# Two output projections of a two-layer trunk as three fp32r products, with weights split by Pool and expert reads moved

## What is computed

```
def diff_attend(q, k, v, lam):
    s = jnp.einsum('cbhqd,cbhkd->cbhqk', q, k)
    p = jax.nn.softmax(s, axis=-1)
    a = p[0] - lam * p[1]
    return jnp.einsum('bhqk,bhkd->bhqd', a, v)

def finish(o):                          # layer 0
    o = rms_norm(o, subln_g) * (1.0 - lambda_init)
    return o.transpose(0, 2, 1, 3).reshape(b, n, D_MODEL) @ w_o

y_lat = o.transpose(1, 0, 3, 2, 4).reshape(b, n, D_MODEL) @ w_o    # layer 1

x = x + gate * y ; h = modulate(rms_norm(x)) ; x = x + gate2 * moe_ffn(h)
```

## Time and profile before

| | |
|---|---|
| median of 3 runs | 1168.38 us (1167.69 to 1175.12) |
| the profiled execution | 1169.04 us, span 1167.2 us |
| mean granted TensorE clock | 0.942 |
| PE busy | 979.8 us, 84% |
| DVE, ACT, POOL busy | 410.1, 365.0, 217.7 us |
| transferred | 321.68 MB, mean 276 GB/s |

### The profile page before, as it was taken

One profiled execution on the slowest core, in us unless ns is written; L12 is line 12 of the kernel. 1 busy time (PEld: TensorE's weight loads), 2 busy tenths in 40 slices (PEclk: granted clock), 3 DMA queues, 4 the chain that ended last, 5 costly groups with the idle time before them and its releaser, 6 DMA issues.

```text
span 1167.2 us, 24449 instructions
## 1 busy us (share of the span) xinstructions
PE 979.8 (84%) x9618; PEld 664.6 (57%) x9619; DVE 410.1 (35%) x840; ACT 365.0 (31%) x777; POOL 217.7 (19%) x329
## 2 busy tenths in 40 slices
PE   4899999988799979799899659999999677996651
PEld 1577777544455655467676447887555545773331
DVE  1533330357843532122222273312853621221113
ACT  3532222456831222122222354223851210220011
POOL 0000000000000034244344301910000132442221
PEclk9899999989999999899999969999999898998786
DMA  9866664998230658999999467223527789999982
GB/s 339 280 225 223 223 216 175 337 362 302 105 161 36 235 213 359 423 418 424 426 421 416 173 240 177 75 72 112 249 75 313 303 336 420 401 423 423 426 374 114
DMA packets 92962, 321.68 MB, mean 276 GB/s; under 512 B 21289, under 2 KB 33234, under 8 KB 80610
## 3 DMA queue, kind: packets, MB, share of 16 engines
q1 hardware_dynamic: 85026, 305.00, 67.7%
q0 software_dynamic: 7008, 12.62, 3.0%
q10 hardware_dynamic: 864, 3.15, 0.7%
HBM read 313.28 MB, written 13.99 MB: 280 GB/s over the span
## 4 chain that ended last, share of the span: by engine, by line
PE 67%; DMA 16%; DVE 6%; issue 5%; ACT 3%; SPq 1%; POOL 1%; POOLq 0%; DVEq 0%; ACTq 0%
PE ps L1947 22%; PE ps L1713 21%; DMA expert_sets<-in_moe_w_up_dram 12%; PE ps L1868 7%; PE ps L1610 5%; PE ps L1634 4%; PE ps L1768 2%; DMA ring<-in_ada_w_dram 2%; PE ps L1795 1%; PE ps L1824 1%; DMA expert_rows<-moe,scatter_idx 1%; DMA val<-expert_rows 1%; PE ps L1651 1%; PE ps L1746 1%; ACT hT L951 1%
## 5 line engine op out<-in xcount | busy, mean ns | idle before, releaser
L1947 PE MATMUL ps<-expert_sets,moe 128*32 128x256 f32 x6304 | 368.1, 393 | 82.8 <-DMA expert_sets<-in_moe_w_up_dram 42.0
L1947 PEld LDWEIGHTS ps<-expert_sets,moe 128*32 128x32 f32 x6304 | 248.2, 114 | 201.9 <-issue 102.0
L1537 DVE STREAM_TRANSPOSE moe<-moe 128x256 f32<-128x256 f32 x70 | 45.7, 654 | 301.3 <-PE ps L1947 283.8
L1713 PE MATMUL ps<-w_high,x_high 128*128 128x512 f32 x352 | 142.2, 404 | 6.8 <-DVE x_low L489 5.1
L1713 PE MATMUL ps<-w_high,x_low 128*128 128x512 f32 x352 | 139.1, 395 | 0.0
L1713 PE MATMUL ps<-w_low,x_high 128*128 128x512 f32 x352 | 139.0, 395 | 0.0
L1090 ACT ACTIVATE moe<-ps 128x128 f32<-128x128 f32 x68 | 18.9, 277 | 308.5 <-PE ps L1947 304.1
L476 DVE TENSOR_TENSOR w_low<-ring,w_high 128x2048 fp32r<-128x2048 f32 x24 | 57.0, 2383 | 133.1 <-ACT w_high L473 133.1
L759 POOL MEMSET moe<- 128x128 f32 x2 | 0.4, 204 | 541.7 <-PE ps L1894 541.7
L783 POOL DMA_INDIRECT expert_rows<-moe,scatter_idx x74 | 75.8, 1024 | 82.8 <-POOL scatter_idx L820 55.2
L1713 PEld LDWEIGHTS ps<-w_high,x_high 128*128 128x128 f32 x352 | 67.2, 191 | 30.7 <-issue 17.6
(11 more groups left out here) (241 smaller groups left out, 1115.8 us busy)
## 6 DMA issues: line engine op xcount, KB each, us to landing
expert_sets<-in_moe_w_down_dram SPq DMA_DIRECT2D x32, 2048.0 KB, 21.8
expert_sets<-in_moe_w_gate_dram SPq DMA_DIRECT2D x30, 2048.0 KB, 17.1
expert_sets<-in_moe_w_up_dram SPq DMA_DIRECT2D x30, 2048.0 KB, 22.8
ring<-in_ada_w_dram SPq DMA_DIRECT2D x16, 2048.0 KB, 8.1
ring<-in_diff_w_qkv_dram SPq DMA_DIRECT2D x6, 2048.0 KB, 8.7
ada_late<-in_ada_w_dram SPq DMA_DIRECT2D x6, 2048.0 KB, 12.1
ring<-in_na_w_qkv_dram SPq DMA_DIRECT2D x6, 2048.0 KB, 8.8
val<-expert_rows SPq DMA_DIRECT2D x12, 512.0 KB, 4.5
```

The costliest lines, as they stand in the source:

```text
L1537: dve.transpose(blk_inT, blk_in[b].rearrange("p (j k) -> p k j", k=KC)).then_inc(m_xt[l], 1)
L1713: mm = pe.matmul(ps[:, n % 2], x_part[:, k, tok], w_part, start=(k == 0 and i == 0), stop=(k == KC - 1 and i == 2))
L1947: mm = pe.matmul(ps[g * SLOTS:(g + 1) * SLOTS, bank, 0:n_out], lhs_T[:, k, :], weights(k, g), start=(k == 0), stop=(k == n_chunks - 1), sk ...
```

## The change

In both layers the product with w_o becomes three fp32r products for each chunk. POOL splits each strip of w_o in halves: a copy to wo_high (fp32r, over expert set 0) and a subtraction into w_low (in place, over the ring). In layer 0 it starts behind the last modulation products, in layer 1 behind the last QKV product. The heads are split too: in layer 0 ACT's copy writes heads_high, and DVE's new heads_low writes x_low from the same bank, one tile ahead; PE may turn the next tile only when heads_low is through. In layer 1 scale_out gets a rounding copy and a subtraction for each pair of heads. As wo_high and heads_high lie where expert 0's weights go, SP reads expert 0 behind the last products of the projection, in both layers, ahead of expert 2. The softmax of layer 0's first half isn't divided by its sum: the combine is e0 + (lam * s0 / s1) * e1, one wide DVE operation instead of two, and the factor 1 / s0 goes into the head's norm by four small operations on the statistics. No other stage is changed.

```
+        wo_high = over("wo_high", SET_KB[0], [P, 2, KC, STRIP], F32R)
+        heads_high = over("heads_high", SET_KB[0] + 32, [P, KC, TILES * P], F32R)
+        o_low = over("o_low", H_KB, [P, KC, SEQ], F32R)
+        first_sums = stat[:, 3]
@@ SP, load_experts
                     expert_weights(l, w, 1, 1)
+                for w, value in ((0, 2 * NT[l] - 1), (1, 2 * NT[l]), (2, 2 * NT[l])):
+                    sp.wait_ge(s_wm[l], value)
+                    expert_weights(l, w, 0, 0)
                 for w, used, value in ((0, s_wm, 2 * NT[l] - 1), (1, s_wm, 2 * NT[l])):
@@ SP, behind layer 0's QKV and behind layer 1's
-            for w, used, value in ((0, s_ada, 2 * ADA - 1), (1, s_ada, 2 * ADA), (2, s_adt, 2 * ADA)):
-                sp.wait_ge(used, value)
-                expert_weights(0, w, 0, 0)
...
-            for w in range(3):
-                if w == 2:
-                    sp.wait_ge(s_qt[1], N_QK[1])
-                expert_weights(1, w, 0, 0)
+            sp.wait_ge(s_qt[1], N_QK[1])
@@ POOL: called at its start with 0, and with 1 behind the bias masks
+            def split_projection(l):
+                for hf in range(2):
+                    st = at[l]["wo", hf]
+                    wait_strip(pool, l, st)
+                    if l == 0:
+                        pool.wait_ge(s_ada, 2 * ADA - 1 + hf)
+                    else:
+                        pool.wait_ge(s_qm[1], len(qkv_jobs[1]))
+                    for half in range(2):
+                        ks = slice(half * KC // 2, (half + 1) * KC // 2)
+                        pool.tensor_copy(wo_high[:, hf, ks], strip(l, st)[:, ks]).then_inc(s_wos, 1)
+                        pool.wait_ge(s_wos, 8 * l + 4 * hf + 2 * half + 1)
+                        pool.tensor_tensor(w_low[:, hf, ks], strip(l, st)[:, ks], wo_high[:, hf, ks], ALU.subtract) \
+                            .then_inc(s_wos, 1)
@@ ACT, exps and turned_out
-                                           accum_out=att[:, u % 3, 4 + cc:5 + cc]).then_inc(s_ex[0], 1)
+                                           accum_out=first_sums[:, 8 * t + h:8 * t + h + 1] if cc == 0 else att[:, u % 3, 5:6]) \
...
-                        dst = hT[:, 4 * hf:4 * hf + 4, t * P:(t + 1) * P]
+                        dst = heads_high[:, 4 * hf:4 * hf + 4, t * P:(t + 1) * P]
@@ DVE, probs
-                        step(dve.reciprocal(a[:, 6:8], a[:, 4:6]))
+                        step(dve.reciprocal(a[:, 7:8], a[:, 5:6]))
-                        step(ts(p1, p1, a[:, 7:8], lam[:, 5:6], ALU.mult, ALU.mult))
-                        stt(p0, p0, a[:, 6:7], p1, ALU.mult, ALU.add).then_inc(s_pr, 1)
+                        step(stt(a[:, 6:7], a[:, 7:8], first_sums[:, 8 * t + h:8 * t + h + 1], lam[:, 5:6], ALU.mult, ALU.mult))
+                        stt(p0, p1, a[:, 6:7], p0, ALU.mult, ALU.add).then_inc(s_pr, 1)
@@ DVE, head_means and invert_roots
+                        step(dve.reciprocal(first_sums[:, cols], first_sums[:, cols]))
+                        step(tt(stat[:, 1, cols], stat[:, 0, cols], first_sums[:, cols], ALU.mult))
+                        step(tt(stat[:, 1, cols], stat[:, 1, cols], first_sums[:, cols], ALU.mult))
...
-                        step(dve.reciprocal(stat[:, 3, cols], stat[:, 2, cols]))
+                        step(dve.reciprocal(stat[:, 2, cols], stat[:, 2, cols]))
+                        step(tt(stat[:, 3, cols], stat[:, 2, cols], first_sums[:, cols], ALU.mult))
@@ DVE, scale_out
+                        high = heads_high[:, g, 0:SEQ]
+                        step(dve.tensor_copy(high, o_lat[:, g]))
+                        tt(o_low[:, g], o_lat[:, g], high, ALU.subtract).then_inc(s_olo, 1)
@@ DVE, projection of layer 0: heads_low(0) ahead of the loop, then
+                def heads_low(m):
+                    t = TILES_OF[0][m]
+                    for hf in range(2):
+                        dve.wait_ge(s_ohi, 2 * m + hf + 1)
+                        ks, cols = slice(4 * hf, 4 * hf + 4), slice(t * P, (t + 1) * P)
+                        stt(x_low[:, ks, cols], ps[:, 4 + hf].rearrange("p (k t) -> p k t", t=P), subln[:, 0:1],
+                            heads_high[:, ks, cols], ALU.mult, ALU.subtract).then_inc(s_olo, 1)
...
                 for m in range(NT[l]):
+                    if l == 0 and m + 1 < NT[0]:
+                        heads_low(m + 1)
@@ PE, turn_out and project_out
-                            pe.wait_ge(s_oc[l], 2 * (m - 1) + hf + 1)
+                            pe.wait_ge(s_olo, 2 * (m - 1) + hf + 1)
...
-                            mm = pe.matmul(ps[:, j % 2], heads_T, strip(l, at[l]["wo", hf])[:, k, :],
-                                           start=(k == 0), stop=(k == KC - 1))
+                            high, low = wo_high[:, hf, k, :], w_low[:, hf, k, :]
+                            for i, (x_part, w_part) in enumerate(((heads_high, high), (heads_high, low), (heads_low, high))):
+                                mm = pe.matmul(ps[:, j % 2], x_part[:, k, tok], w_part, start=(k == 0 and i == 0),
+                                               stop=(k == KC - 1 and i == 2))
...
-                    pe.wait_ge(s_oe[1], HEAD_PAIRS)
+                    pe.wait_ge(s_olo, 2 * NT[0] + HEAD_PAIRS)
```

32 lines of the change are left out of this document (20 added, 12 removed).

## The result

The changed kernel takes 1186.58 us (median of 6 runs, 1182.37 to 1189.23), against 1168.03 us for the kernel before (6 runs): the ratio is 1.0146, with a 95% interval of 1.0121 to 1.0171. It is slower by 1.5%, or 18.5 us. The prediction said 1177 us and gave 1158 to 1189. The profiled execution took 1189.23 us, its span is 1187.3 us, 20.1 more than that of before, and the mean granted clock of TensorE is 0.920 instead of 0.942. It is the slowest of the six executions and has the lowest mean clock of them (0.922 to 0.935 in the others), so what its trace shows is a little more than the change costs as a rule.

A forecast was written before the change was run, and what follows sets the result against it. No engine was taken to bind everywhere: TensorE carried 67% of the span, and transfers bound the expert stages. Layer 0's +6.5 us and layer 1's +1.8 us summed to +8.3 us, so 1177 us, range 1158 to 1189.

The forecast's parts named there:

- fold: Layer 0's attention: DVE's wide scaling replaced by a one-column operation, -2.3 us (bounds 0 and -6).
- heads_low: Start of layer 0's projection: the first product waits for the heads' second part, +2.1 us (bounds 1 and 3).
- reads: Expert stages: expert 0's reads moved behind the projection, +3 us in each layer (bounds 0 and 8).
- POOL against DVE: Layer 0's attention: DVE operations with two SBUF inputs wait for whole POOL split instructions, +14.8 us (0 to +18).
- The rival by which the engines hardly exclude each other: POOL and DVE in both layers: the waits vanish or shrink to 5 and 1 us; 1159 or 1165 us, chance 0.22.
- Layer 1 on POOL's side: Layer 1 before its projection: router multiplication and scale_out wait for POOL's split, +3.5 us (bounds 0 and 9).
- the tail: Layer 1, ahead of the first projection product: the last group's copy and subtraction lie open, +0.9 us.
- The products: Output projections: three-product form gains 0.173 us a chunk, -11.1 us in layer 0, -5.6 us in layer 1, all on the path.
- The rival with 12 us a layer: Expert stages: transfers bind, each layer pays up to 14.9 us instead of 3; 1201 us, chance 0.13 including one layer alone.
- the likeliest case: Whole kernel: time as forecast, 1168 to 1186 us, chance 0.55.
- the rival in which one layer is bound by its reads: Expert stage of one layer: transfers bind there alone, 1189 us; shares the chance 0.13 with both layers binding.
- no change: Whole kernel: neither faster (under 1156.7 us) nor slower (over 1180.1 us), chance 0.58.

The follow-up runs named there:

- Experiment 2: Kernel before, with expert 0's reads late and POOL's whole copies and subtractions of the projection weights added, results unused: 1192.90 us, ratio 1.0210.
- layer 0 only: Changed kernel with layer 1 put back as before (plain fp32 projection, no POOL split, early expert read): 1182.99 us, ratio 1.0138.
- experiment 7: 24 idle-filling products in layer 0, added to the changed kernel (the 70.1): 1181.35 us, ratio 1.0129; added to the kernel with 128x512 POOL instructions: 1166.07 us, ratio 0.9978.
- the pieces: Changed kernel with POOL's instructions cut to 128x512, one-column factor with one tensor input: 1166.61 and 1166.68 us; layer 0 alone: 1169.40 (128x256), 1169.61 (128x512, two-input factor).
- the fold alone: Kernel before with only layer 0's first softmax sum moved into the head norm, one wide multiplication less per unit: 1166.48 us, ratio 0.9978.
- the one-input factor: Changed kernel with the one-column factor as an instruction with one tensor input and two scalar pointers, instead of two tensor inputs: 1181.01 us, ratio 1.0098.

## Why the prediction came out as it did

The same stretches, forecast and measured in the profiled executions (microseconds against before):

| step | forecast | measured | off by |
|---|---|---|---|
| layer 0 up to the first product (fold, POOL, heads_low) | +14.6 | +14.3 | -0.3 |
| layer 0's products | -11.1 | -9.0 | +2.1 |
| plan, up to the first gather | 0 | +2.9 | +2.9 |
| gather to layer 1's first product (reads, POOL, scale_out) | +7.4 | +9.6 | +2.2 |
| layer 1's products | -5.6 | -3.6 | +2.0 |
| behind them (reads) | +3 | +4.9 | +1.9 |
| before any of it | 0 | +0.9 | +0.9 |
| sum | +8.3 | +20.0 | +11.7 |

*POOL against DVE* was the step in dispute, and it holds, in mechanism and nearly in size: copies of 1.89 us (forecast 2.0) and subtractions of 4.51 (4.8), a one-column operation that waits for a whole subtraction, a combine that waits for the next copy. Unit 21's combine ends at 303.5 (305.1), which is 12.2 us later than before when both are counted from unit 19's maximum, where 14.8 was forecast. Experiment 2 has POOL's part by itself: +12.8 us up to the first product. The column of layer 0 only (70.8), the changed kernel's (70.0) and that of experiment 7 (70.1) against the pieces' 56.6 to 58.6 put it at 11 to 14 us. What the pieces keep over the fold's 52.9 is 4 to 6 us: 0.8 of it lies up to unit 21's combine, 1.9 is heads_low's longer wait (3.03 instead of 1.18; forecast +2.1), and the rest seems to go with the granted clock behind unit 31, 0.69 to 0.88 there against the fold's 1.00. So the -0.3 of the table's first row is in part luck: POOL's waits were forecast 1 to 3 us too large, and the clock was left out. The rival by which the engines hardly exclude each other fell.

The Trainium skill (SBUF — State Buffer, section SBUF: two separate sides) also names a DVE operation in a two-port mode as one that needs the shared pair. Experiment 2's wide scaling with one SBUF input (3.35 instead of 0.55 us) and the copy of layer 1's heads (2.17 us in the changed kernel, 0.30 without a collision) did wait, as they would by that rule; in which mode they ran no trace here shows. The one-column form with one tensor (0.27) didn't wait.

*Layer 1 on POOL's side* was sized too low: +3.5 was forecast, +4.4 with the tail, and between the router's first multiplication and the first product it measured +5.1 (experiment 2, without the tail) and +5.9 (the changed kernel, with it; the tail is 0.8). The step that failed is which operations meet POOL. The forecast had the second router multiplication wait for a copy and scale_out(0) for a subtraction, with 1.5 us inside DVE's idle time. The multiplication met the third subtraction in full: 4.16 us instead of 0.29 (chain, 840.60), the first one 1.45 instead of 0.28, and none of these 5.0 us was covered. scale_out's two operations on PSUM took their 0.41 and 0.43 us while POOL worked, and only the new copy behind them waited (2.17), which cost nothing.

*The products* have the forecast price at the granted clock that the forecast took from QKV. At a clock of 1.00 throughout, layer 0's projection takes 54.6 and 54.7 us (forecast 54.1), layer 1's 25.5 (forecast 25.2). The step that failed is the sentence that all of the gain is on the path "since PE has no gap there": it looked for gaps inside the projection only. The gap of 3.03 us ahead of it is the wait for heads_low, which was itself forecast, but not that the clock falls behind it. This term costs 1.5 to 1.9 us in layer 0 (0.4 with pieces of 256). In layer 1 the changed kernel loses 1.7 us in the same way, but there the record speaks against the gap as the whole cause: the wait for o_low is 1.77 us (1.0 before) in all seven kernels with the new form in layer 1, and the clock fell behind it in three of them (projection 27.2) and stayed at 1.00 in four (25.5). No kernel filled that gap, and what decides stays open.

*The plan's 2.9 us* was in no term. It is the clock, 0.50 between 405 and 410: the 38 fillers take 10.64 us of the chain instead of 8.30, and the products of the router's logits ahead of them 1.89 instead of 1.07. But it isn't the change's: the fold alone (22.4) and the late reads with POOL (22.4) have part of it, the one-input factor and both kernels with pieces of 512 in both layers (20.6) have none. It stands in one execution and not in another kernel with the same stage. What decides it stays open.

*The reads* cost +3.1 and +3.8 us by themselves (forecast 3 and 3), by the mechanisms that were named: company for the gathers in layer 0, a read that finds the queue busy in layer 1. The rival with 12 us a layer fell. In layer 1 the nine kernels with late reads take 243.7 to 249.7 us behind the first gather, mean 247.8, the five without, the kernel before among them, 243.4 to 245.7, mean 244.7: 3.1 apart, so the profiled 4.6 of the changed kernel is in part chance.

The sum came 11.7 us short in the profiled execution, 9.6 in the medians (1186.58 against 1177). The direction and the terms in dispute were right; what was missing are small losses of 1 to 3 us, all of one sign. Some 6 of the 11.7 us are the granted clock, which had no term (the 2.9 and most of the 2.1 and 2.0 in the table), and 4 to 5 of these come and go between executions of kernels that are the same in that stage. A range that reached to 1189 held the time, while the likeliest case's own range, up to 1186, just missed it. That the range held it is in part luck: its upper end was the rival in which one layer is bound by its reads, and that rival fell. By the prediction's own limit of 1180.1 the kernel is slower, which it had given a chance of 0.32; it gave 0.58 to no change.

Is there a version that beats both? The change with POOL's work in pieces, the one-input factor and the fillers has a ratio of 0.9978 (0.9957 to 0.9998), and the fold alone has the same, 0.9978 (0.9961 to 0.9995). Both are faster than before by 0.2%, hardly more than nothing. With pieces the rest of the change adds up to about zero: the products' 13 to 16 us are eaten up by 4 to 5 us of heads_low, short waits and clock, less 3 of the fold, and by 8 to 14 us of reads, clock and layer 1's tail (the last columns of the table).

## What to carry to other kernels

An idle engine isn't a free one: before work is given to POOL beside a busy DVE, list the DVE operations that will meet it, and cut POOL's instructions to the length of a DVE instruction, since DVE waits for the one under way and no longer. Where a change makes TensorE wait some 3 us just ahead of a long run of products, price that run's beginning at the lower granted clock, or fill the gap; but see what else the fillers hold up. And compare two traces stage by stage between marks, for identical work ahead of a change differed by up to 7 us from one profiled execution to another.

## What the runs showed of the hardware

- While POOL ran a copy or a subtraction from SBUF to SBUF, DVE operations with two SBUF inputs (one-column 3.08 to 3.41 us instead of 0.22, 128x96 2.90, 128x512 2.33), a wide scaling (128x512, 3.35 instead of 0.55) and a wide copy (128x256, 2.17 instead of 0.30) stood until POOL's instruction ended. A reciprocal of one or two columns (0.15), a one-column scaling with two scalar pointers (0.27) and operations that read PSUM (a maximum, 1.21; a multiplication with one PSUM and one SBUF input, 0.43) did not. That a one-tensor operation waits when it is wide and not when it has one column was in no row of the kernel before.
- A POOL operation of 128x2048 takes 1.89 us for a copy to fp32r and 4.51 for a subtraction; in pieces of 128x512, 0.61 and 1.27, with 1.15 and 1.67 where DVE's turn comes first.
- Around a gap of 3.03 us ahead of layer 0's projection the granted clock fell in all of seven kernels (0.50 and 0.66 in the 5 us stretches shown), 39 products of 128x512 took 10.48 us, and with the gap filled the clock was 1.00 in all of three. Behind a gap of 1.77 us in layer 1 it fell in three of seven, behind gaps of 1.18 and 0.98 us in none. The fall in layer 0 is not as long in all: the projection took 55.1 us in the kernel with pieces of 256 and 56.2 to 56.6 in the others.
